# A decoder step: expert slots of 32 tokens by four experts, and sample attention by chunks with their own maximum

## The reference

```
h = x*(1+scale1)+shift1;  q,k,v,B,C,u = h @ w_in
A1 = softmax(q1 k1^T/8 + bias); A2 = softmax(q2 k2^T/8 + bias)      # 4 heads
o  = RMSNorm((A1 - lambda*A2) v)
x  = LayerNorm(alpha*x + gate1*([o, B*conv3(C*u)] @ w_out)); h2 = x*(1+scale2)+shift2
PEER(h2): per token and each of 8 heads: 2 x 128 scores -> best 16 of each
          -> 256 sums -> best 16 experts, softmax g;
          f = sum over 128 experts of g*gelu(U[e].h2)*V[e]            # rows of 1024
y  = LayerNorm(alpha*x + gate2*f)
```

## Time and profile before

| | |
|---|---|
| median of three runs | 4429.04 us |
| the profiled execution | 4432.87 us, its span 4431.2 us |
| condition, project, conv | 0 to 495 us |
| prompt attention | 495 to 716 us |
| sample attention | 716 to 1231 us |
| mix | 1232 to 1412 us |
| PEER | 1412 to 4431 us, first gather issued at 1497.7 |
| busy: PE, DVE, ACT, POOL | 3462.9, 2442.9, 1350.9, 1495.7 us |
| granted TensorE clock, mean | 0.889 of 2.4 GHz |

### The profile page before, as it was taken

The page is one execution under the profiler, slowest core; times in us unless marked ns, Lnnn a source line. Parts: engine busy times, 40 slices in busy tenths (PEclk is TensorE's granted clock), DMA queues, the critical chain, the costliest instruction groups (busy, mean ns, idle before and its releaser), DMA issues. The chain is left out here.

```text
span 4431.2 us, 48459 instructions
## 1 busy us (share of the span) xinstructions
PE 3462.9 (78%) x12230; PEld 1663.3 (38%) x12230; DVE 2442.9 (55%) x5891; ACT 1350.9 (30%) x3845; POOL 1495.7 (34%) x1599
## 2 busy tenths in 40 slices
PE   5999665777766578687887888888878878788786
PEld 4446344544422233233333333333333333333332
DVE  1102354333245475857756855854864864874785
ACT  0110132333200233333333333343343333333333
POOL 0000000222300233444543544454443554454454
PEclk7999777888788889898999899899889899999989
DMA  8121603787734598998998998998998999999898
GB/s 330 47 46 29 22 1 104 273 287 281 262 142 144 226 376 311 379 387 355 421 396 340 418 399 329 416 420 335 417 410 330 398 416 376 380 421 375 363 418 344
DMA packets 245916, 1342.83 MB, mean 303 GB/s; under 512 B 47321, under 2 KB 60858, under 8 KB 94149
## 3 DMA queue, kind: packets, MB, share of 16 engines
q0 software_dynamic: 164352, 1174.49, 65.9%
q1 hardware_dynamic: 63456, 144.12, 10.6%
q10 hardware_dynamic: 17892, 21.83, 1.5%
HBM read 1319.30 MB, written 20.97 MB: 302 GB/s over the span
## 5 line engine op out<-in xcount | busy, mean ns | idle before, releaser
L1502 PE MATMUL psum<-sb_ring,sb_diag 128*128 128x512 f32 x4224 | 2089.9, 650 | 573.7 <-PEq L62 567.1
L1633 DVE CUSTOM_DVE_ANT_0 sb_ring<-sb_ring,sb_h_tiles 128x1024 f32<-128x1024 f32 x1056 | 1269.0, 1224 | 840.6 <-DMA sb_ring<-in_uv,sb_index_stage 808.7
L1502 PEld LDWEIGHTS psum<-sb_ring,sb_diag 128*128 128x128 f32 x4224 | 853.1, 208 | 1791.5 <-issue 1791.0
L1476 POOL DMA_INDIRECT sb_ring<-in_uv,sb_index_stage x1056 | 1256.5, 1190 | 628.6 <-POOLq L62 334.5
L1575 ACT ACTIVATE sb_gelu<-sb_dots 128x1 f32<-128x1 f32 x1056 | 210.9, 200 | 1153.9 <-ACTq L62 1136.6
L804 POOL DMA_DIRECT2D sb_v_pages<-in_cache_v x256 | 135.1, 528 | 1086.1 <-POOLq L62 1063.8
L1474 POOL COPY sb_index_stage<-sb_experts 128x4 uint32 (+1 forms) x264 | 93.7, 355 | 1052.5 <-POOLq L62 1050.5
L1580 ACT ACTIVATE sb_diag<-sb_ident,sb_expert_w 128x128 f32<-128x128 f32 x1024 | 411.1, 401 | 33.3
L1577 ACT ACTIVATE sb_expert_w<-sb_gelu,sb_gates 128x1 f32<-128x1 f32 x1056 | 311.0, 295 | 114.4 <-ACT sb_gelu L1575 3.8
L1520 PE MATMUL psum<-sb_w_pq,sb_h2T 128*128 128x512 f32 x576 | 259.3, 598 | 1.3 <-PEq L62 1.3
L866 PE MATMUL psum<-sb_ident,sb_k_pages 128*128 128x128 f32 x1024 | 153.3, 316 | 52.9 <-PEq L62 52.8
(11 more groups left out here) (212 smaller groups left out, 2459.2 us busy)
## 6 DMA issues: line engine op xcount, KB each, us to landing
sb_v_pages<-in_cache_v POOLq DMA_DIRECT2D x256, 256.0 KB, 4.4
sb_k_pages<-in_cache_k SPq DMA_DIRECT2D x256, 256.0 KB, 4.1
sb_w_ada<-in_w_ada SPq DMA_DIRECT2D x12, 2048.0 KB, 17.5
sb_ring<-in_uv,sb_index_stage POOLq DMA_INDIRECT x1056
sb_w_pq<-in_w_pq SPq DMA_DIRECT2D x4, 2048.0 KB, 17.1
sb_w_qkv<-in_w_in SPq DMA_DIRECT2D x3, 2048.0 KB, 19.4
sb_w_bcu<-in_w_in SPq DMA_DIRECT2D x12, 512.0 KB, 5.6
sb_h_tiles<-h_scratch SPq DMA_DIRECT2D x9, 512.0 KB, 8.0
```

Of the source, the lines that this page charges most:

```text
L1476: pool.indirect_dma_start(ring[:, slot, :], None, uv, bass.IndirectOffsetOnAxis(ap=stage[:, c % 4, s:s + 1], axis=0))\
L1502: ins = nc.tensor.matmul(psum[:, n, :], diag[:, slot, :], ring[:, slot, D + n * BANK:D + (n + 1) * BANK], start=(c == 0 and s == 0), stop= ...
L1633: dot = nc.vector.tensor_tensor_reduce(ring[:, slot, 0:D], ring[:, slot, 0:D], h2[:, u], 1.0, 0.0, ALU.mult, ALU.add, dots[:, slot:slot + 1])
```

## The change

It alters `sample_attention` and `peer`. In sample attention every chunk is exponentiated with its own maximum, straight from PSUM; each chunk's value product goes to its own rows of `oc` and is scaled by exp(own maximum - sample's maximum) when the sample's eight chunks are there. There are three slots for key chunks and three for value chunks, and the 64 chunks are one written-out sequence without a hardware loop; keys of chunk k+1 are turned, chunk k scored, chunk k-1's probabilities turned, chunk k-2 multiplied with values. The new tokens' scores ride with the sample's last chunk. Waits are on rising counts.

In PEER a slot holds 32 tokens by four experts, so a tile has four token groups of 32 places, still 128 gathers of 128 rows. The weights go into a 128 x 32 matrix, and V is multiplied in four products of 256 columns, each in its own column group of 32, into one PSUM bank per token group (two in turn). Per token group ACT copies h2's 32 rows to four places (`fourfold`) and collects four 32 x 256 results. Expert numbers and gates are written in the new layout by sixteen small DVE instructions each, POOL's index copies go, and the first tile's choice is finished before its first gather.

```diff
 sample_attention:
+    DEEP = 3
+        kp, vp = sbuf "k_pages", "v_pages" [P, DEEP, CH, AW]
+                def turn_keys(k):      # waits k_land[k % 3], kT_done of chunk k-1
+                def score(k):
+                    if k >= 1: pe.wait_ge(T["exp_ready"], k)
+                    for h in range(H):
+                        ins = nc.tensor.matmul(psum[head(h), SCORE, :], q_all[:, b, h, :], kpT[:, k % 2, h, :], ...)
+                def values(k):
+                    if k >= 2: pe.wait_ge(T["o_copied"], k - 1)
+                    for j in range(CH):
+                        for h in range(H):
+                            ins = nc.tensor.matmul(psum[head(h, M), VALUE + k % 2, 0:DV], pT[:, k % 2, j, h, :], ...)
+                for k in range(STEPS + 2):
+                    if k + 1 < STEPS: turn_keys(k + 1)
+                    if k < STEPS: score(k)
+                    if 1 <= k <= STEPS: turn_probs(k - 1)
...
+                    if k >= 2: values(k - 2)
+                def exps(k):           # ACT
+                    act.wait_ge(T["max_ready"], k + 1)
+                    step(nc.scalar.activation(ex[:, k % 2, :], psum[:, SCORE, :], ACT.Exp, bias=nmx[:, b % 2, c:c + 1],
+                                              accum_out=z[:, b % 2, c:c + 1]))
+                for k in range(STEPS + 2):   # DVE: copy_keys(k+1), maxima(k), copy_probs(k-1), copy_out(k-2)
...
+                    if c == 2 and 1 <= b < NB: heights(b - 1)
+                    if c == 4 and 1 <= b < NB: combine(b - 1)
 peer:
-            for c in range(16):
-                select(0, 0, c)
-            part_chosen(0)
+            for c in range(30):
+                select(0, 0, c)
+            begin()
+            beside(0, 0, "none", 1)
...
-                            src = e_all[:, ds(index(t), 1), c * GROUP:(c + 1) * GROUP]
-                            step(nc.gpsimd.tensor_copy(stage[:, c % 4, :], flat(src)))
...
-                        for n in range(2):
-                            ins = nc.tensor.matmul(psum[:, n, :], diag[:, slot, :], ring[:, slot, D + n * BANK:D + (n + 1) * BANK], ...)
+                        for q in range(COPIES):
+                            ins = nc.tensor.matmul(psum[q * NS:(q + 1) * NS, g % 2, 0:QUARTER], fw[:, slot, :],
+                                                   ring[:, slot, D + q * QUARTER:D + (q + 1) * QUARTER],
+                                                   start=(n == 0), stop=(n == NS - 1), skip_group_check=True)
...
+                        nc.scalar.activation(fw[:, slot, :], fold[:, 0:NS], ACT.Copy, scale=wgt[:, slot:slot + 1])
+                        if 4 <= n < 8 and not (g == 0 and isinstance(t, int) and t == 0):
+                            collect((g - 1) % COPIES, n - 4)
+                        if n in (12, 16, 20, 24) and t is not None:
+                            if g + 1 < COPIES: fourfold(u, g + 1, (n - 12) // 4)
...
+                        for g, q in pieces(t):
+                            step(nc.vector.scalar_tensor_tensor(out=experts[dst, u, g, :], in0=ef[0][src, q], ...))
```

More of the change, by code:

```diff
@@ L775, in sample_attention @@
+        k_land, k_free, v_land, v_free = ([sem(f"sa_{x}_{what}{u}") for u in range(DEEP)]
+                                          for x in "kv" for what in ("land", "free"))
         dve_c, act_c = sem("sa_dve"), sem("sa_act")
-        EXPS = NCH // 2
-        def exp_cols(p):
-            return slice(p * 2 * BANK, (p + 1) * 2 * BANK + (NT if p == EXPS - 1 else 0))
+        KT, SCORE, TURN, VALUE, FRESH = 0, 4, 5, 6, DV
         def head(h, n=NS):
             return slice(h * NS, h * NS + n)
[L789 to L801, removed]
+        def load(eng, cache, slots, land, free, k):
+            u = k % DEEP
+            pages = [eng.value_load(pt[0:1, k * CH + g:k * CH + g + 1], min_val=0, max_val=POOL - 1) for g in range(CH)]
+            if k >= DEEP:
+                eng.wait_ge(free[u], k // DEEP)
@@ L853, in _ @@
                                            start=(t == 0), stop=(t == NT - 1))
                 ins.then_inc(T["bias_psum"], 1)
[L855 to L861, removed]
+                def turn_keys(k):
+                    u = k % DEEP
+                    pe.wait_ge(k_land[u], (k // DEEP + 1) * 16 * CH)
@@ L934, in _ @@
-                samples(pe, body)
-                for u in range(2):
-                    take(pe, T[f"v_free{u}"])
-                    take(pe, T[f"k_free{u}"])
+                            ins = nc.tensor.matmul(psum[head(h, M), bank, 0:DV], pT[:, k % 2, j, h, :],
+                                                   vp[:, u, j, h * DV:(h + 1) * DV],
+                                                   start=(j == 0), stop=(j == CH - 1 and not last), skip_group_check=True)
+                    ins.then_inc(v_free[u], 1)
@@ new lines, in values @@
+                    if last:
+                        pe.wait_ge(T["pnT_ready"], b + 1)
+                        for h in range(H):
+                            ins = nc.tensor.matmul(psum[head(h, M), bank, 0:DV], pnT[:, h, :],
+                                                   v[0:NS, TILES, h * DV:(h + 1) * DV],
+                                                   start=False, stop=True, skip_group_check=True)
+                        ins.then_inc(T["o_psum"], 1)
+                    else:
+                        pe.wait_ge(v_free[u], k // DEEP + 1)
+                        pe.sem_inc(T["o_psum"], 1)
@@ L939, in _ @@
+                pe.wait_ge(T["o_all_ready"], 1)
+                combs = rows[:, 2 + AW:].rearrange("p (b n) -> p b n", b=NB)
+                for h in range(H):
+                    for b in range(NB):
+                        ins = nc.tensor.matmul(psum[0:NS, KT + h, 0:DV], combs[head(h), b, :], o_all[head(h), b, :],
+                                               start=(b == 0), stop=(b == NB - 1), skip_group_check=True)
+                ins.then_inc(T["sum_ready"], 1)
             @block.scalar
@@ L1398, in run @@
             tidy()
-        def enters(t, c):
-            return c % (GROUPS // PARTS) == 0 if isinstance(t, int) and t == 0 else c == 0
         def index(t):
```

577 lines of the change are left out of this document (283 added, 294 removed).

## The result

The changed kernel takes 4158.35 us (median of four runs, 4143.18 to 4159.68) against 4431.8 us of the kernel before on the same chip: a ratio of 0.937, interval 0.934 to 0.941, so 273 us were saved where 293 were predicted. The profiled execution is the fastest of the four (4143.18 us, span 4141.2); against the profile of before its span is 290.0 us shorter. The steps are compared on these two profiles; the 15 us between this execution and the median come back under the total.

The account below looks back on a forecast made before the run. Sample attention was taken as bound by its loop's form and two slots, PEER by PE's order holding slots during score making, elsewhere by DMA. Gains of 139 and 154 us from 4432.87 gave 4140, range 4070 to 4280.

Parts of the forecast that it names:

- A gather's products, 0.64 us: PEER: eight 256-column products in four column groups take PE 0.64 us a gather, in place of 1.76.
- rival C: TensorE stays at its low clock: 8.4 us a chunk, PEER tiles stay 350 us, total 4523; chance 0.07.
- A tile, 327 us: PEER: a tile falls from 350.5 us to the DMA floor, 325.7, plus 1.3 not covered; bounds 322 and 350.5.
- First tile, +58 and -50.6: PEER's start: choosing all eight heads before the first gather costs 58 us; tile 0 without its crowding gains 50.6.
- PEER's sum: PEER: +58 - 50.6 - 7 x 23.5, +3 for copies, gives -154 us; bounds -194 and +28.
- Sample attention, -139: Sample attention: DMA becomes the bound at 5.40 us a chunk; end at 1092 against 1231.4; bounds -166 and -60.
- 329 + 8: Sample attention: 61 chunks at 5.40 us make 329, plus 8 for late value slots and POOL's queue at the start.
- 9 + 9: Sample attention's end: 9 us for the last chunk's steps, 9 for the last sample's combination.
- The total: Whole kernel: -139 - 154 = -293 us on the profiled execution's 4432.87, giving 4140; chance 0.57.
- A: PEER: PE still holds the slots while making scores, half the dip stays, 340 us a tile, total 4244; chance 0.13.
- B: Sample attention: the chain of score, maximum and exponent bounds a chunk at 7 us, total 4242; chance 0.12.
- D: PEER: column groups don't run side by side with V, 1.76 us a gather, tile 350, total 4322; chance 0.04.

Follow-up runs that it names:

- sa_only: New sample attention with the old PEER (whole functions exchanged), against the kernel before: 4288.87 us, ratio 0.968.
- two_slots: The changed kernel with two slots for key and for value chunks in place of three: 4198.31 us, ratio 0.947 to the kernel before.
- one_group: The changed kernel with a gather's four products all in column group 0, so not side by side: 4318.71 us, ratio 0.974 to the kernel before.

## Why the prediction was right

*What bounds it.* Right for the kernel before: sample attention was bound by its form and its two slots (`sa_only`, `two_slots`; their parts only as far as given above), PEER by PE's time per slot beside the scores (`one_group`). For the changed kernel it was right in PEER and wrong in sample attention, where DMA did not become the bound (below).

*A gather's products, 0.64 us.* Measured 0.64 at the high clock, the value worked out from `score`. That the clock would then fall was not in the forecast's own terms, only in rival C, which had 1.07: 1.08 us is what many gathers pay, and the mean over the run is 1030.9/1056 = 0.98 us.

```profile
L1490 PE MATMUL psum<-sb_ring,sb_fold_weighted 128*32 128x256 f32 x8448 | 1030.9, 585 | 1405.1 <-PEq L62 1300.3
```

*A tile, 327 us.* Measured 328.96. The floor had been put at 417 GB/s, 325.7 us, with 1.3 for what is not covered; at the 421 that the search stretches move it is 322.6, so some 6 us are not covered. In the tile shown most of them lie in the last pieces, 70 x (1 - 389/421) = 5.3 us: there the forecast saw PE stand some 8 us and counted on the eight slots to make it up, which they did in part. The 421 goes against the 358 GB/s that the prediction quoted; the Trainium skill's "HBM Reference" (Specifications) has the fitting sentence, that a core streaming alone measures about 425 GB/s; the best slices here, 421, agree with it.

*First tile, +58 and -50.6.* The first gather came 1412.75 - 1087.53 = 325.2 us after sample attention's last copy, against 1497.70 - 1230.85 = 266.9: +58.4. From it to the first collection lie 342.5 us instead of 383.6, and from the last collection to the end 83.2 instead of 96.2: -41.1 and -12.9, together -54.0, where -50.6 and +3 stood, -47.6 together. The mark itself has moved: a tile's last group is now collected five slots into the next tile, so only the sum can be compared.

*PEER's sum.* +58.4 - 54.0 - 7 x 21.58 = -146.7 against -154. The missing 7 us are the tiles' 2 us each (13.5 in all), partly made up at the ends (6.4).

*Sample attention, -139.* From the first key transposes to the end it took 1231.4 - 736.7 = 494.7 us and takes 1088.1 - 732.9 = 355.2: -139.5. The other 3.8 us are an earlier start of this one execution; in the ten other profiles the key transposes start at 735.2 to 742.4. The size came out, but not by the step that was to give it. The forecast let DMA set 5.40 us a chunk. From 840 us on PE waits for no landing, neither before its key transposes (here) nor before its value products, and the chunks follow each other as PE's own work lets them:

```profile
L835 PE MATMUL psum<-sb_ident,sb_k_pages x672: 272/273/329, 841.1 to 1052.9; 128*128 128x128 f32 x168
its engine sat idle before it (us, times) until:
  issue: 25.4, 42
  PE psum L883: 10.6, 32
  DVE sb_k_pagesT L1005: 4.1, 5
```

```profile
1000.51 1.94 PE L835 MATMUL psum<-sb_ident,sb_k_pages 128*128 128x128 f32 x16 [0.33 <-PE psum L883]
...
1005.36 1.94 PE L835 MATMUL psum<-sb_ident,sb_k_pages 128*128 128x128 f32 x16 [0.33 <-PE psum L883]
```

That is 4.85 us, all but 0.33 of it PE's own instructions. With the new tokens' turn, which makes one gap of a sample 6.2 us, and DVE's combination, which makes two of 5.3, a sample's eight chunks take 41.05 us, time after time: 5.13 a chunk. POOL's loads of values in turn wait 103.5 us of this stretch (840 to 1055) for PE to be through with a slot. The DMA engines are close behind: 2.097 MB at the 421 GB/s of PEER's search would be 4.98 us a chunk, and their share is 1.01, so a full share did not show here that the transfers set the time. The other terms were off too, and cancelled: the last values land 1069.1 - 732.9 = 336.2 us after the first transposes, where 329 + 8 stood, but 61 chunks of 5.13 are 313, so the start and the trailing values cost some 23 us, not 8; the 19.0 us of waits for keys all lie in this start. That -139 and -139.5 agree so closely is luck. Behind the last landing 19.0 us follow, where 9 + 9 stood, and these are divided otherwise:

```profile
1069.09 1.06 PE L883 MATMUL psum<-sb_v_pages,sb_probsT 128*8 128x128 f32 x32 [0.70 <-DMA sb_v_pages<-in_cache_v]
...
1076.17 11.32 PE L915 MATMUL psum<-sb_o_samples,sb_row_consts 32*32 32x128 f32 x64 [5.69 <-DVEq L88]
```

The last chunk is at its value products when the values land and needs 1.5 us more, not 9. The "32 small products" are 64 instructions and take 11.3 us alone, at a granted clock of 0.50; with DVE's steps and the copy the combination, 1070.5 to 1088.1, is 17.6 us, not 9.

*The total.* 4140 for the profiled execution, which took 4143.18. The median lies 15 us higher. Part of that lies ahead of PEER: in the seven other profiles with the same sample attention up to that point the head sums begin at 1079.2 to 1086.6, 3 to 10 us after the 1076.17 above. So that 4140 meets this execution to 3 us is partly luck; against the median it is 18 us short. What differs from run to run there was not looked into, and no profile of a run at the median exists.

*The rivals.* A did not come: the share stays at 0.98 to 1.01 beside the pieces, and of the dip the 5 us above are left. B came in part, as far as the waits show: the order of the engines sets a chunk, by PE's own work more than by the chain of score, maximum and exponent, at 5.13 us and not 7, below the 5.40 of the forecast. D is what `one_group` makes by hand: 4322 was worked out for it and 4318.71 measured (its +28 leaves out the 6 us for the first landing that the forecast's -50.6 has; with them it would be 4328). C came by half: in PEER the clock is 0.62 where it was 0.92, and a piece that took 3.60 us takes 4.2 to 4.8. It costs little, because the rival had put all at the low level: 24.7 us for two groups. Here the low level stands where PE has least to do (0.55 from 2540 to 2725), and the levels are mixed beside the pieces (0.74 and 0.81): one piece and its four gathers keep PE busy 4.65 + 1.07 + 0.64 + 1.08 = 7.4 us, and four gathers need 4 x 2.57 = 10.3 us of DMA. In sample attention the dense order held 0.99.

## What to carry to other kernels

Where slots of a ring go back only when one engine is through with them, its time per slot decides the transfers beside its other work; make that work short (here by four column groups with a smaller stationary tile) rather than speed up what already waits. Give a stream of transfers one slot more than the steps that hold one, and see by the waits for landings whether it was enough and whether the transfers are still the bound; a DMA share of 1.0 alone does not tell. What a new layout needs before it can start is paid once, in full, with nothing beside it; splitting that start into parts gives back a good part, provided that no other queue is filled up behind the parts.

## What was not expected

The new PEER runs with the DMA engines full at a mean TensorE clock of 0.62 (1755 to 4058 us), while the same kernel with nearly three times the product time per slot (`one_group`) was granted 0.92 over the same seven tiles (1786 to 4238 us). Only the column groups differ, so the lighter products went with the lower clock, and 0.64 us became 1.08 for many gathers; it still paid, since both are below the 1.77 us of one column group.

A quarter fewer bytes gave a tile 33 us of the 82 that its bytes were worth, with the DMA engines as fast as before where their share was full. And in sample attention PE waited for no landing in 215 us (840 to 1055) although the DMA share was full. There the order of the engines sets 5.13 us a chunk; by the 4.98 above, an estimate, some 10 us of the stage could be had from it before the transfers bind.
